# Key counts as logarithms in the mask, and attention's values in two products a head, in a two-block transformer kernel

## What is computed

```python
# fox: causal softmax with a decay between query t and key s
s = einsum('bhqd,bhkd->bhqk', q, k) * scale + cq[..., :, None] - c[:, :, None, :]
p = softmax(where(kpos <= qpos, s, NEG_INF));   out = p @ v
# dilated: three branches (window, dilation) = (128,1), (512,4), (2048,16), ALiBi penalty,
# each normalised, then mixed with weights softmax(log-denominators)
o, lse = branch(q, k, v, window, dilation)
out = sum(softmax(lses) * os)
```

## Time and profile before

| | us |
|---|---|
| median of three runs | 2436.36 (2435.85 to 2439.2) |
| the profiled execution's own time | 2437.05 |
| its span | 2434.8 |
| attention: first scores to last values | 42.6 to 260.9 |
| chain that ended last | PE 94%, ACT 2%, DVE 2%, DMA 2% |

### The profile page before, as it was taken

How to read it: one execution, slowest core, us unless ns; L and a number is a source line. 1 busy time by engine, 2 the same in 40 slices (tenths; PEclk the granted TensorE clock), 3 DMA queues, 4 the chain that set the end, 5 groups by cost and what they waited for, 6 DMA issues and landing times.

```text
span 2434.8 us, 35667 instructions
## 1 busy us (share of the span) xinstructions
PE 2407.2 (99%) x13533; PEld 2189.7 (90%) x13533; DVE 1776.7 (73%) x3391; ACT 1185.2 (49%) x2193; POOL 565.0 (23%) x372
## 2 busy tenths in 40 slices
PE   9999999999999999999999999999999999999998
PEld 7788988999999999999999998887888889888887
DVE  7876767998998886899999988787785336433323
ACT  6455466478788885333333345445322223322222
POOL 3222074133333541455555510000000000000000
PEclk9999999999999999999999999999999999999999
DMA  5111355699999999999999972222573322232331
GB/s 191 53 62 44 122 165 169 234 320 350 345 331 345 388 403 362 411 412 412 412 408 407 410 286 81 83 87 88 187 260 128 104 87 96 95 103 88 108 100 35
DMA packets 193114, 533.89 MB, mean 219 GB/s; under 512 B 16712, under 2 KB 65896, under 8 KB 190768
## 3 DMA queue, kind: packets, MB, share of 16 engines
q1 hardware_dynamic: 151472, 380.60, 43.5%
q0 software_dynamic: 41472, 151.01, 16.3%
HBM read 480.09 MB, written 51.46 MB: 218 GB/s over the span
## 4 chain that ended last, share of the span: by engine, by line
PE 94%; ACT 2%; DVE 2%; DMA 2%; issue 0%; DVEq 0%; SPq 0%; ACTq 0%
PE P L1359 29%; PE P L1361 29%; PE P L1360 29%; PE P L1724 2%; DMA hdram<-HID 1%; PE P L1366 1%; ACT wh L2545 1%; PE P L1639 0%; PE P L1638 0%; PE P L1637 0%; PE P L1790 0%; PE P L1616 0%; PE P L1617 0%; ACT OM L2755 0%; PE P L1615 0%
## 5 line engine op out<-in xcount | busy, mean ns | idle before, releaser
L1359 PE MATMUL P<-XH,wh 128*128 128x512 f32 (+2 forms) x2272 | 833.6, 367 | 0.0
L1361 PE MATMUL P<-XH,wl 128*128 128x512 f32 (+2 forms) x2272 | 817.4, 360 | 0.0
L1360 PE MATMUL P<-XL,wh 128*128 128x512 f32 (+2 forms) x2272 | 817.0, 360 | 0.0
L2545 ACT ACTIVATE wh<-raw 128x1024 fp32r<-128x1024 f32 x458 | 482.3, 1056 | 399.7 <-PE P L1361 399.7
L1834 DVE TENSOR_TENSOR wl<-raw,wh 128x1024 fp32r<-128x1024 f32 x422 | 511.7, 1220 | 86.5 <-ACT wh L2545 84.4
L1361 PEld LDWEIGHTS P<-XH,wl 128*128 128x128 f32 x2272 | 427.4, 188 | 47.7
L1359 PEld LDWEIGHTS P<-XH,wh 128*128 128x128 f32 x2272 | 427.7, 188 | 43.4 <-issue 1.9
L1360 PEld LDWEIGHTS P<-XL,wh 128*128 128x128 f32 x2272 | 428.1, 188 | 42.7 <-issue 1.9
L1359 PE MATMUL P<-AH,wh 128*128 128x368 f32 (+1 forms) x1024 | 337.5, 330 | 1.1 <-DVE AL L1834 1.1
L1360 PE MATMUL P<-AL,wh 128*128 128x368 f32 (+1 forms) x1024 | 336.8, 329 | 0.0
L1361 PE MATMUL P<-AH,wl 128*128 128x368 f32 (+1 forms) x1024 | 336.7, 329 | 0.0
(11 more groups left out here) (344 smaller groups left out, 3382.1 us busy)
## 6 DMA issues: line engine op xcount, KB each, us to landing
raw<-wts SPq DMA_DIRECT2D x211, 512.0 KB, 3.6
raw<-ut SPq DMA_DIRECT2D x128, 512.0 KB, 7.3
raw<-vt SPq DMA_DIRECT2D x128, 512.0 KB, 11.7
hdram<-HID SPq DMA_DIRECT2D x64, 384.0 KB, 6.1
HI<-hdram SPq DMA_DIRECT2D x32, 768.0 KB, 13.2
gdram<-GS SPq DMA_DIRECT2D x23, 1024.0 KB, 9.7
GI<-gdram SPq DMA_DIRECT2D x16, 1472.0 KB, 11.5
AWC<-adat SPq DMA_DIRECT2D x64, 256.0 KB, 5.0
```

What stands on the lines that cost most here:

```text
L1359: e.matmul(bank, wh[:, w], H, start=start, stop=False)
L1360: e.matmul(bank, wh[:, w], L, start=False, stop=False)
L1361: return e.matmul(bank, wl[:, w], H, start=False, stop=stop)
L2545: return e.activation(dst, src, ACT.Copy)
```

## The change

**Counts.** The mask of the dilated heads, MDB, holds minus the logarithm of the count instead of zero (the score bank holds the negated score, so this multiplies the exponential by the count). It is now float32, the count table CNT is gone, `normal` loses its multiply-and-sum (L1988), and ACT's exponential makes the row sum for all heads.

**Values.** VX keeps for each block of keys and head 64 high columns and 64 low columns side by side. For 15 of the 16 heads, a block of keys then takes one product with 128 stationary columns (high and low by PTH) and one with 64 (high by PTL), which writes rows 0 to 63 of P6 alone. Rows 64 to 127 hold the low columns' share, and have to be added: ACT copies rows 0 to 63 to MS (the buffer TB[5]), DVE adds rows 64 to 127 into MS, ACT copies MS to MH one turn of the loop later (`values_high`), and POOL writes ML = MS - MH. The last head takes three products of 64 columns a block, and ACT and DVE as before.

**Order.** The two numbers in `attend()` become 1.23 and 1.18 for all turns; `state["values"]`, on which the output projection's tiles wait in the list, counts at `values_high`.

```diff
-            yield 1.4 if n < 34 else 1.05
+            if 0 <= n - 6 < ns and steps[n - 6][2] == 3:
+                yield ("values_high", *steps[n - 6][:2])
+                state["values"] += 1
+            yield 1.23
...
                 yield ("values", g, h, at[n - 5], v_at[g])
-                state["values"] += 1
...
-            yield 1.35 if n < 34 else 1.05
+            yield 1.18
...
-        CNT = at("CNT", F + 13, [128, T], F32)
-        MDB = at("MDB", F + 15, [128, T], BF16)
+        MDB = at("MDB", F + 13, [128, T], F32)
...
-        VV = [[at(f"VV{g}{i}", F + 80 + 4 * g + 2 * i, [128, 4, 128], F32R) for i in range(2)] for g in range(2)]
+        VX = [at(f"VX{g}", F + 80 + 4 * g, [128, 4, 2, 2, 64], F32R) for g in range(2)]
...
+        MS = TB[5]
...
PE:
                 if v:
-                    p.wait_ge(s_ml, v)
+                    p.wait_ge(s_mix, 3 * v - 1)
...
-                    e.matmul(d, vh[:, kb, :], key_row(PTH, v, kb), start=kb == 0, stop=False)
-                    e.matmul(d, vh[:, kb, :], key_row(PTL, v, kb), start=False, stop=False)
-                    m = e.matmul(d, vl[:, kb, :], key_row(PTH, v, kb), start=False, stop=kb == 3)
+                    d = slice(kb * 128, T)
+                    if v < 15:
+                        def wide():
+                            return e.matmul(P[6][:, d], both[:, kb, h, :, :].rearrange("p a b -> p (a b)"),
+                                            key_row(PTH, v, kb), start=kb == 0, stop=kb == 3)
+                        def narrow():
+                            return e.matmul(P[6][0:64, d], both[:, kb, h, 0, :], key_row(PTL, v, kb), start=False,
+                                            stop=False)
+                        if kb < 3:
+                            wide()
+                            narrow()
+                        else:
+                            narrow()
+                            m = wide()
...
DVE, normal:
-                if dilated(g):
-                    v.wait_ge(s_const, 4)
-                    step(e.tensor_tensor_reduce(out=p_[:, 0:kw], in0=p_[:, 0:kw], in1=CNT[:, (3 - qb) * 128:T],
-                                                scale=1.0, scalar=0.0, op0=ALU.mult, op1=ALU.add,
-                                                accum_out=st[:, c + 2:c + 3]).then_inc(s_v, 1))
-                    own()
...
DVE, values:
-                v.wait_ge(s_mh, 2 * g + h + 1)
-                tt(ML[rows, place(g), :], P[6][rows, :], MH[rows, place(g), :].bitcast(F32),
-                   ALU.subtract).then_inc(s_ml, 1)
+                n = 2 * g + h
+                v.wait_ge(s_mix, 3 * n + 1)
+                if n < 15:
+                    tt(MS[rows, :], P[6][64:128, :], MS[rows, :], ALU.add).then_inc(s_mix, 1)
...
ACT, soft:
-                if dilated(g):
-                    e.activation(dst, src, ACT.Exp, bias=st[:, j:j + 1], scale=-1.0).then_inc(s_exp, 1)
-                else:
-                    e.activation(dst, src, ACT.Exp, bias=st[:, j:j + 1], scale=-1.0,
-                                 accum_out=st[:, j + 2:j + 3]).then_inc(s_exp, 1)
+                e.activation(dst, src, ACT.Exp, bias=st[:, j:j + 1], scale=-1.0,
+                             accum_out=st[:, j + 2:j + 3]).then_inc(s_exp, 1)
...
ACT, values and values_high:
-                copy(MH[rows, place(g), :], P[6][rows, :]).then_inc(s_mh, 1)
+                copy(MS[rows, :] if n < 15 else MH[rows, place(g), :], P[6][0:64, :]).then_inc(s_mix, 1)
+            def values_high(g, h):
+                if n < 15:
+                    c.wait_ge(s_mix, 3 * n + 2)
+                    copy(MH[rows, place(g), :], MS[rows, :]).then_inc(s_mix, 1)
...
POOL:
+            def values_high(group, h):
+                if (group, h) != (7, 1):
+                    g.wait_ge(s_mix, 3 * (2 * group + h + 1))
+                    e.tensor_tensor(ML[rows, place(group), :], MS[rows, :], MH[rows, place(group), :].bitcast(F32),
+                                    ALU.subtract).then_inc(s_ml, 1)
```

More of the change, by code:

```diff
@@ L1633, in values @@
                 p.wait_ge(s_tr[tv % 2], tv // 2 + 1)
-                vh, vl = VV[g % 2]
+                both = VX[g % 2]
                 for kb in range(4):
-                    d = P[6][:, kb * 128:T]
-                    e.matmul(d, vh[:, kb, :], key_row(PTH, v, kb), start=kb == 0, stop=False)
-                    e.matmul(d, vh[:, kb, :], key_row(PTL, v, kb), start=False, stop=False)
-                    m = e.matmul(d, vl[:, kb, :], key_row(PTH, v, kb), start=False, stop=kb == 3)
+                    d = slice(kb * 128, T)
[12 more added lines that the diff above has]
+                            m = wide()
+                    else:
+                        e.matmul(P[6][0:64, d], both[:, kb, h, 0, :], key_row(PTH, v, kb), start=kb == 0, stop=False)
+                        e.matmul(P[6][0:64, d], both[:, kb, h, 1, :], key_row(PTH, v, kb), start=False, stop=False)
+                        m = e.matmul(P[6][0:64, d], both[:, kb, h, 0, :], key_row(PTL, v, kb), start=False,
+                                     stop=kb == 3)
                 m.then_inc(s_val, 1)
@@ L2005, in values @@
                 rows = slice(64 * h, 64 * h + 64)
-                v.wait_ge(s_mh, 2 * g + h + 1)
-                tt(ML[rows, place(g), :], P[6][rows, :], MH[rows, place(g), :].bitcast(F32),
-                   ALU.subtract).then_inc(s_ml, 1)
+                n = 2 * g + h
+                v.wait_ge(s_mix, 3 * n + 1)
+                if n < 15:
+                    tt(MS[rows, :], P[6][64:128, :], MS[rows, :], ALU.add).then_inc(s_mix, 1)
+                else:
+                    v.wait_ge(s_ml, 15)
+                    tt(ML[rows, place(g), :], P[6][0:64, :], MH[rows, place(g), :].bitcast(F32),
+                       ALU.subtract).then_inc(s_ml, 1)
             def mixed(m, half):
@@ L2655, in v_copy @@
                 c.wait_ge(s_fox_v, 1)
-                if g >= 2:
-                    c.wait_ge(s_vt, g - 1)
-                copy(TB[6 - g % 2][:, :], P[qkv_home(g, 2)][:, :]).then_inc(s_vcopy, 1)
+                c.wait_ge(s_vt, g)
+                copy(TB[6][:, :], P[qkv_home(g, 2)][:, :]).then_inc(s_vcopy, 1)
             def v_turn(g, t):
@@ L2663, in v_turn @@
                     c.wait_ge(s_val, 2 * (g - 1))
-                copy(VV[g % 2][0][:, :, :], P[4 + t % 2][:, :].rearrange("p (b c) -> p b c", b=4)).then_inc(s_vh, 1)
+                copy(VX[g % 2][:, :, :, 0, :],
+                     P[4 + t % 2][:, :].rearrange("p (b h c) -> p b h c", b=4, h=2)).then_inc(s_vh, 1)
             def soft(n, g, h, qb):
@@ L2918, in _ @@
             work = {f.__name__: f for f in (
-                high, gained, near, counts, square, root, gain, table, norm, forget, qk_split, v_copy, v_turn, soft, turn, values, subkeys, query, key,
+                high, gained, near, counts, square, root, gain, table, norm, forget, qk_split, v_copy, v_turn, soft, turn, values, values_high, subkeys, query, key,
                 token, gate, gate_turn, weigh, grid, hidden, rows, extra_turn, dots_end, mod_load, mod_part, rotation, square2, both_gains,
@@ L2937, in low @@
                         g.wait_ge(s_fill, last["fill"])
+                    if "mix" in last:
+                        g.wait_ge(s_ml, last["mix"])
                     if "part" in last:
@@ L2960, in fill @@
                 last["fill"] = n
+            def values_high(group, h):
+                rows = slice(64 * h, 64 * h + 64)
+                if (group, h) != (7, 1):
+                    g.wait_ge(s_fill, last["fill"])
+                    g.wait_ge(s_low_p, last["low"])
+                    if group or h:
+                        g.wait_ge(s_ml, 2 * group + h)
+                    g.wait_ge(s_mix, 3 * (2 * group + h + 1))
+                    e.tensor_tensor(ML[rows, place(group), :], MS[rows, :], MH[rows, place(group), :].bitcast(F32),
+                                    ALU.subtract).then_inc(s_ml, 1)
+                    last["mix"] = 2 * group + h + 1
             def mod_part(n):
@@ L2994, in gather_v @@
                     ap=(SIX if extra else SI)[:, k:k + 1], axis=0)).then_inc(d_row[n % 6], 16)
-            work = {f.__name__: f for f in (low, fill, mod_part, gather, gather_v)}
+            work = {f.__name__: f for f in (low, fill, values_high, mod_part, gather, gather_v)}
             for name, *a in timeline():
```

42 lines of the change are left out of this document (24 added, 18 removed).

## The result

The kernel after takes 2441.3 us (median of 22 runs, 2436.11 to 2446.93), the kernel before 2437.27 (22 runs): ratio 1.0017, interval 1.0012 to 1.0023. It is 4 us slower, 0.17% and so under the 0.2% that the prediction set as its bound; the forecast was 2426.5. The profiled execution is its fastest, 2436.11 us with a span of 2434.0, so what the median has on top of it is not in this trace.

A forecast was written before the change was run, and what follows sets the result against it. PE was taken to bound the kernel, busy in 2407.2 of 2434.8 us. The terms -9.3 - 4.1 + 1.6 + 1.9 = -9.9 us gave a median of 2426.5, likeliest range 2420 to 2431, wide range 2420 to 2446.

The forecast's parts named there:

- Part 1: Values in 15 heads: four of twelve products fall away, 0.62 us a head, 9.3 us gained on PE.
- M: Theory for the values' products: the array empties where 128 and 64 columns take turns.
- Part 2: Dilated heads, 60 to 112 us: DVE loses L1988, PE's idle time falls from 4.6 to 0.5, 4.1 us gained.
- Part 3: Row sums and MS to MH copies on ACT, subtractions on POOL: costed at nothing, hidden by idle time.
- Part 4: The list's new numbers: 1.6 us lost at attention's start, 1.9 us at its last turning.
- even: Middle of attention: a fox step gets 0.21 us more tiles and 0.16 less of values; a dilated one loses 0.39.
- The slow stretch I keep as it is: The stretch of 3.4 us at granted clock 0.50, at 57.6 us, was assumed to stay unchanged.
- What attention gains should reach the end: Behind attention PE runs nearly without a gap, its loads starting when buffers come free, so gains should last.
- first rival: Array empties at 92 turns between 128 and 64 columns: 14.7 us, 2441.2; chance 0.19 full price, 0.08 half.
- The range's lower end: 2420 us, given for the bounds of parts 2 to 4 without turns of mode.
- the second: Dilated stretch keeps its waits, POOL's hold and ACT's chain eating DVE's relief: 2431 to 2439 us, chance 0.17.
- The sentence that would have shown the whole wrong: Wrong if attention's PE time doesn't fall, or a wait on DVE's scaling behind POOL takes the place of L1988.

The follow-up runs named there:

- old numbers: The kernel after with the list's numbers of before (1.4 and 1.35 for the first 34 turns, then 1.05): 2438.57 us.
- quarters: Each of POOL's weight splits issued as four pieces of 256 columns: 2434.71 us on the kernel after, 2433.23 us on the kernel before.
- values alone: The kernel after, with the counts multiplied and summed on DVE as before and the list's numbers of before: 2440.73 us.
- counts alone: The kernel before with the counts in the mask and nothing else, three products a block: 2433.06 us.
- the next profile: The kernel after measured once more, unchanged, for a second profile: 2443.47 us.

## Why the prediction was wrong, point by point

**Part 1, the products (-9.3): right, and M is out.** One head's values on PE in the kernel after, answering:

```profile
160.35 0.39 PE L1641 MATMUL P<-PTH,VX 128*128 128x512 f32 x1
160.57 0.39 PE L1645 MATMUL P<-PTL,VX 128*64 128x512 f32 x1
160.81 0.34 PE L1641 MATMUL P<-PTH,VX 128*128 128x384 f32 x1
...
161.45 0.28 PE L1641 MATMUL P<-PTH,VX 128*128 128x128 f32 x1
161.56 0.41 PE L1368 MATMUL P<-ident,T 128*128 128x128 f32 x2
```

160.35 to 161.56 is 1.21 us (1.24 predicted), and 128 and 64 columns follow each other 0.22 to 0.24 us apart, as equal neighbours did. The drain that the Trainium skill ("TensorEngine Tiling (Array Packing)", "Key Properties") puts at a change of mode costs no time that this trace shows. All heads are as short: from the first start to the last, a head's values take 1.09 to 1.18 us in each kernel with two products and 1.74 to 1.83 in each with three, 9.7 us less over the 15 heads, where 9.3 were forecast. The Rest column, rougher, has -8.4 to -11.4 in the kernels with two products, but for the two at the old numbers.

**Part 2, the counts (-4.1): the time by itself came out, 4.2, the idle time only in part; in the sum it bought nothing.** By itself it took 2.9 us of waiting away and left 1.7, where 0.5 was forecast; that the medians differ by 4.2 is in part luck. The counts and the quarters took the same waits away, those for the scaling, so, as far as these runs tell, they were held scalings, which a DVE with less to do lets pass. In the kernel after, the new holds and the chain behind the forget gate put 5.9 us into the stretch where 0.5 was forecast. DVE didn't fall to 31.8 but to 36.5 of 52 us; with quarters, which shorten the holds, it is 33.5.

**Part 3, "costed at nothing": the step that failed.** The values alone cost 3.4 us by the medians instead of giving 9.3, 12.7 us off. The text priced POOL's subtraction by its own length, at most 1.39 us (1.30 measured), and found cover for 15 such holds. It didn't ask what is queued behind it on POOL while it waits for MH. Two rows of the kernel after, POOL's groups from 48 to 265 us, give the answer in their last column:

```profile
L2972 POOL TENSOR_TENSOR wl<-raw,wh 128x1024 fp32r<-128x1024 f32 x20 | 48.0, 2402 | 16.5 <-ACT wh L2563 15.4 <-POOL wl L2972 0.2
L2998 POOL TENSOR_TENSOR ML<-T,MH 64x512 fp32r<-64x512 f32 x15 | 19.4, 1296 | 126.0 <-ACT MH L2563 99.3 <-PE P L1363 26.7
```

POOL waits 126 us in front of ML, and 12 of the 15 times a split behind it had its wh 4.7 us or more before it could start. What holds a scaling then is the split, 2.4 us, not ML's 1.3. This cost the kernel after 5.7 us, the idle time that quarters take away (1.79 at 77 us and five times 0.77 or more).

**Part 4, the ends (+3.5): nearly right; the middle, "even", was the second failed step.** The last turning waited 1.88 us (1.9 forecast), the start lost 0.6 us and 0.3 at a turning behind it instead of 1.6. But the part counted tiles a step and not what the new order sets side by side: it brought a head's copy MS on ACT close behind the forget gate's copy, which has a wait of its own, and that cost 4.1 us. The old numbers remove that wait, and so does moving the forget gate's piece. Undoing the numbers gave 2.7 us on the kernel after, though the old ones bring the held scalings out more.

**"The slow stretch I keep as it is": a term left out.** In the ledger, stretches at granted clock 0.50 cost from 0 to 7.6 us, by the estimate. In attention the kernel after had one of 3.4 us in its fastest execution and three with 17.1 us together in the next profile, two of them at the waits of 2.6 and 4.1 us; that accounts for 5.9 of the 6.5 us between the two. Its median is 5.2 us above its fastest run, before's 1.6.

**"What attention gains should reach the end": up to a point.** Up to 830 us each kernel keeps what it had gained or lost at attention's end, within 0.1 us. From 830 to 945 us they then move by -0.6 to +3.8 us against before, and not by how far ahead they are: the values alone, level with before, lose 2.0 us, and the counts alone, 5.3 us ahead, gain 0.6. All eight that lose more than 1 us have a stretch of 3.4 us at the granted clock 0.50 that starts between 853 and 863 us, and only one of the other five has it; before has none there. What decides it stays open.

The sum for the fastest execution: -9.3 for the products and +8.2 of idle time, -1.1 against -0.85 measured at attention's end. By PE's waits the +8.2 are: -4.6, all old waits of the dilated stretch; +5.7, the held scalings; +4.1, the copy behind the forget gate; +2.8, start and end; and 0.3 at one wait for scores at 235 us. The forecast had -4.1 and +3.5 of these, and nothing for the 9.8 us of the second and third. From that execution to the median it is another 5.2 us. That the median, 2441.3, is nearly the first rival's 2441.2 is chance: its mechanism cost nothing that a trace shows. The range's lower end was added up wrongly, too: the bounds of parts 2 to 4 give 2424 and not 2420; and part 1's bound speaks of four products of 128 columns a head where the list has two. Neither bears on the miss.

**The rivals:** the second, that POOL holds DVE, was the mechanism, with 2439 as its worst; it was given 0.17, because it was looked for in the dilated stretch only, and at ML's own price. The sentence that would have shown the whole wrong, a wait on the scaling behind POOL, is what the waits of the kernel after read. Still open is when a stretch at half clock starts and how long it lasts: behind a first wait of about 2.5 us, kernels had none, one of 3.4 or one of 6.8 us.

## What to carry to other kernels

Before work is moved to an idle engine, ask what it waits for there and what stands behind it in that engine's queue: an engine that is idle three quarters of the time can still be made late, and the late instruction may be another one, longer than the one that was moved. Where a VectorE instruction lasts as long as the GpSimd one that it starts behind, cut GpSimd's instructions into pieces no longer than VectorE's slack; here that gave 4.1 us to the old kernel and 6.6 to the new one by itself. When the pace of a list changes, look at which pieces with a wait of their own come to stand next to each other, not only at how much work each step gets. Price the parts of a change alone before adding them up: two parts that remove the same wait pay once, and a part that adds waits can eat another's gain.

## What the runs showed of the hardware

A scaling that starts 0.06 us after a GpSimd subtraction lasts about until that subtraction ends, for both lengths seen: 2.42 us beside 2.39, 0.77 us beside a piece of 0.75 (747 ns in the mean), where alone it takes 0.29. A product with 64 stationary columns between products with 128 costs no more than its moving columns, 0.22 to 0.24 us for 512. Cutting 128x1024 into four pieces of 256 costs GpSimd 18% (2.40 to 2.83 us). At the granted clock 0.50, 512-column products start 0.42 to 0.43 us apart instead of 0.23, so a stretch of 3.4 us costs an estimated 1.7 us of PE's work at most; in attention, two executions of the same kernel had 3.4 and 17.1 us of it.
